# Expert layers of a two-layer mixer: plain fp32 products in column tiles, 16 landing pieces of two rows a partition

## The reference, cut to what matters

```python
N_EXPERTS = 16; EC_FACTOR = 2; D_EXPERT = D_MODEL = 1024

def expert_choice_ffn(h, router, w1, w3, w2):
    B, T, D = h.shape
    cap = max(1, EC_FACTOR * T // N_EXPERTS)
    aff = jax.nn.softmax(jnp.einsum('btd,de->bte', h, router).astype(jnp.float32), -1)
    gate, idx = lax.top_k(jnp.swapaxes(aff, 1, 2), cap)
    xs = jax.vmap(lambda hb, ib: hb[ib])(h, idx)
    hid = jax.nn.silu(jnp.einsum('becd,edf->becf', xs, w1)) * jnp.einsum('becd,edf->becf', xs, w3)
    ys = jnp.einsum('becf,efd->becd', hid, w2) * gate[..., None].astype(h.dtype)
    return jax.vmap(lambda yb, ib: jnp.zeros((T, D), yb.dtype).at[ib.reshape(-1)].add(yb.reshape(-1, D)))(ys, idx)
```

## Time and profile before

| | |
|---|---|
| median of 3 runs | 4865.87 us (4865.85 to 4869.79) |
| span of the profiled execution | 4858.5 us |
| between the two | 7.4 us |
| busy: PE, DVE, ACT, POOL | 86%, 64%, 39%, 10% |
| HBM read | 624.96 MB, 134 GB/s over the span |
| layer 0: first load, first product, last product's end | 717, 783, 1385 us |
| layer 1: the same | 2518, 2571, 3164 us |

### The profile page before, as it was taken

The page is one execution under the profiler, slowest core; times in us unless marked ns, Lnnn a source line. Parts: engine busy times, 40 slices in busy tenths (PEclk is TensorE's granted clock), DMA queues, the critical chain, the costliest instruction groups (busy, mean ns, idle before and its releaser), DMA issues. The chain is left out here.

```text
span 4858.5 us, 70272 instructions
## 1 busy us (share of the span) xinstructions
PE 4160.4 (86%) x28730; PEld 3310.1 (68%) x28730; DVE 3090.2 (64%) x4658; ACT 1887.0 (39%) x2558; POOL 481.2 (10%) x383
## 2 busy tenths in 40 slices
PE   7978876999978887979978999988989958697998
PEld 3855674666657774868854555587878748686877
DVE  6368957888864556656457888855467343574772
ACT  5122324667642312222125666634432222363221
POOL 0011000111101001414100111112000000100000
PEclk9987888999989997979788999999999977799999
DMA  7120026999960211000047999940122221002222
GB/s 274 35 90 26 1 89 244 356 349 370 369 218 34 69 54 57 3 6 3 23 164 283 358 364 361 327 125 1 36 101 94 91 67 37 1 2 70 95 96 78
DMA packets 254463, 658.45 MB, mean 136 GB/s; under 512 B 26884, under 2 KB 108036, under 8 KB 253624
## 3 DMA queue, kind: packets, MB, share of 16 engines
q1 hardware_dynamic: 240256, 614.97, 35.6%
q0 software_dynamic: 9216, 34.66, 2.6%
q10 hardware_dynamic: 4672, 4.33, 0.3%
HBM read 624.96 MB, written 28.41 MB: 134 GB/s over the span
## 5 line engine op out<-in xcount | busy, mean ns | idle before, releaser
L1843 DVE TENSOR_TENSOR w_lo<-w_quarter,w_hi 128x2048 fp32r<-128x2048 f32 x384 | 874.5, 2288 | 199.9 <-ACT w_hi L1766 198.6
L1766 ACT ACTIVATE w_hi<-w_quarter 128x2048 fp32r<-128x2048 f32 x384 | 735.5, 1918 | 378.7 <-DMA w_quarter<-in_moe_w 203.6
L3099 DVE TENSOR_TENSOR w_lo<-ffn_landing,w_hi 128x1024 fp32r<-128x1024 f32 x132 | 161.4, 1225 | 293.3 <-ACT w_hi L3077 293.3
L3051 PE MATMUL ffn_ps<-ffn_inT_hi,w_hi 128*128 128x512 f32 x704 | 276.4, 393 | 9.2 <-DVE w_lo L3099 9.2
L3051 PE MATMUL ffn_ps<-ffn_inT_lo,w_hi 128*128 128x512 f32 x704 | 276.0, 392 | 0.0
L3051 PE MATMUL ffn_ps<-ffn_inT_hi,w_lo 128*128 128x512 f32 x704 | 275.6, 391 | 0.0
L1343 ACT ACTIVATE prob<-score_ps,negmax 128x256 f32<-128x256 f32 (+4 forms) x272 | 166.4, 612 | 233.3 <-DVE negmax L1316 233.0
L1714 PE MATMUL down_ps<-w_hi,hiddenT 128*96 128x512 f32 (+1 forms) x512 | 207.0, 404 | 43.3 <-DVE w_lo L1843 32.1
L1651 POOL DMA_INDIRECT summed_dram<-gains_then_rows,row_token x32 | 118.3, 3696 | 1028.7 <-DVE gains_then_rows L1862 1028.7
L1714 PE MATMUL gate_ps<-w_hi,rowsT 128*96 128x512 f32 (+1 forms) x512 | 205.3, 401 | 12.7 <-DVE w_lo L1843 9.6
L1714 PE MATMUL up_ps<-w_hi,rowsT 128*96 128x512 f32 (+1 forms) x512 | 204.5, 399 | 6.2 <-DVE w_lo L1843 6.1
(11 more groups left out here) (680 smaller groups left out, 9811.3 us busy)
## 6 DMA issues: line engine op xcount, KB each, us to landing
w_quarter<-in_moe_w SPq DMA_DIRECT2D x384, 1024.0 KB, 6.8
ffn_landing<-in_f_w_up SPq DMA_DIRECT2D x88, 512.0 KB, 3.3
ada_landing<-in_ada_w SPq DMA_DIRECT2D x24, 1024.0 KB, 7.3
ada_ring<-in_ada_w SPq DMA_DIRECT2D x24, 1024.0 KB, 5.2
ffn_landing<-in_f_w_down SPq DMA_DIRECT2D x44, 512.0 KB, 3.3
w_landing<-in_od_w_in SPq DMA_DIRECT2D x13, 1024.0 KB, 10.6
w_landing<-in_a_w_in SPq DMA_DIRECT2D x12, 1024.0 KB, 6.0
w_landing<-in_ev_w_in SPq DMA_DIRECT2D x6, 1024.0 KB, 5.7
```

Source lines behind the costliest of these rows:

```text
L1766: nc.scalar.activation(wh[g % NP][:, :, :], land[g % NL][:, :, :], ACT.Copy).then_inc(hi_ready, 1)
L1843: tt(wl[g % NP][:, :, :], land[g % NL][:, :, :], wh[g % NP][:, :, :].bitcast(F32), ALU.subtract) \
L3051: mm = nc.tensor.matmul(ps[c % 4][:, :], w[:, c % NP, cols], h[:, k, :], start=(k + i == 0), stop=(k == KD - 1 and i == 2))
L3099: nc.vector.tensor_tensor(wl[:, c % NP, :], land[:, c % NL, :], wh[:, c % NP, :].bitcast(F32), ALU.subtract).then_inc(split, 1)
```

## The change

- The split is gone, and with it `wh`, `wl`, `hi_part`, `lo_part`, `turned_hi` and `turned_lo`. Products read the landed pieces as plain fp32. xs and hT have one buffer each, written by ACT (`rows_kept`) and DVE (`hidden_kept`).
- Products go in column tiles. For the 64 latent rows, half n of the output columns goes to partitions 64n to 64n + 63, in `out[:, 0:512]`. For the 32 context rows of layer 0, quarter n goes to partitions 32n to 32n + 31, in `out[:, 512:768]`. So hidden, y and the gain lie in that layout ("parts"), y is added by one indirect DMA of 128 half rows, and in layer 0 a second one of 128 quarter rows, with indices `pidx` worked out by DVE.
- 16 landing pieces. 10 in layer 0 and 12 in layer 1 are loaded at once; half of the others lie where nT is and wait for `scored`, half where h is and wait for `h_stored`. Later loads wait for `used`, PE's count of quarters. Their semaphores live through both layers (`landed`, `loaded`).
- A piece's rows are laid out as "(p k) n" instead of "(k p) n": a partition gets two neighbouring rows, 8 KB in one run, and the transposes pick rows and columns with a step of 2 to match.

```diff
+    LW, CW = D // 2, D // 4
+    W = LW + (CW if CR else 0)
+    NL = len(landed)
+    n_turn = nt // 2
+    n_free = NL - 2 * n_turn
...
-                    sp.wait_ge(split, g - NL + 1)
+                    sp.wait_ge(used, g - NL + 1)
-                sp.dma_start(land[g % NL][:, :, :], src.rearrange("(k p) n -> p k n", p=P)) \
+                sp.dma_start(land[g % NL][:, :, :], src.rearrange("(p k) n -> p k n", k=QK)) \
...
-            for g in range(NL):
+            for g in range(n_free):
                 load(g)
...
-            for g in range(NL, len(order)):
+            sp.wait_ge(scored, 1)
+            for g in range(n_free, n_free + n_turn):
                 load(g)
-            sp.wait_ge(y_added, 16 * E)
+            sp.wait_ge(h_stored, 16 * nt)
+            for g in range(n_free + n_turn, len(order)):
+                load(g)
+            sp.wait_ge(y_added, 16 * NS * E)
...
+                scatter(e, 0, lat_rows, slice(0, LW))
+                if CR:
+                    scatter(e, 1, ctx_rows, slice(LW, W))
...
             def quarter(out, v, g):
-                pe.wait_ge(split, g + 1)
-                q, c = order[g][2], g % NP
+                c = g % NL
+                pe.wait_ge(landed[c], 16 * (before[c] + g // NL + 1))
+                q = order[g][2]
                 for kk in range(QK):
                     k = q * QK + kk
...
                     for n in range(2):
-                        cols = slice(n * 512, (n + 1) * 512)
-                        nc.tensor.matmul(out[0:R, cols], v[0][:, k, :], wh[c][:, kk, cols], start=first, stop=False,
-                                         skip_group_check=True)
-                        nc.tensor.matmul(out[0:R, cols], v[0][:, k, :], wl[c][:, kk, cols], start=False, stop=False,
-                                         skip_group_check=True)
-                    for n in range(2):
-                        cols = slice(n * 512, (n + 1) * 512)
-                        mm = nc.tensor.matmul(out[0:R, cols], v[1][:, k, :], wh[c][:, kk, cols], start=False,
-                                              stop=last, skip_group_check=True)
+                        mm = nc.tensor.matmul(out[n * 64:(n + 1) * 64, 0:LW], v[:, k, 0:LR],
+                                              land[c][:, kk, n * LW:(n + 1) * LW], start=(k == 0), stop=(k == KD - 1),
+                                              skip_group_check=True)
+                for kk in range(QK if CR else 0):
+                    k = q * QK + kk
+                    for n in range(4):
+                        mm = nc.tensor.matmul(out[n * 32:(n + 1) * 32, LW:W], v[:, k, LR:R],
+                                              land[c][:, kk, n * CW:(n + 1) * CW], start=(k == 0), stop=(k == KD - 1),
+                                              skip_group_check=True, tile_position=(0, n * 32))
                 mm.then_inc(used, 1)
 
             def turn_hidden(e):
                 pe.wait_ge(hid_ready, e + 1)
...
+                for part in range(NS):
+                    for j in range(LW // P if part == 0 else CW // P):
+                        c = part * LW + j // QK * QK * P + j % QK
+                        mm = nc.tensor.transpose(misc[part][:, j * P:(j + 1) * P], hid[:, c:c + QK * P - 1:QK], ident)
...
-                pe.wait_ge(hid_kept, 2 * f + 2)
+                pe.wait_ge(hid_kept, NS * (f + 1))
+                if f:
+                    pe.wait_ge(y_ready, f)
...
+            def hidden_kept(e):
+                for part, n, r0, r in ((0, 2, 0, LR), (1, 4, LR, CR))[0:NS]:
+                    dve.wait_ge(hid_turned, NS * e + part + 1)
+                    nc.vector.tensor_copy(hT[:, :, r0:r0 + r].rearrange("p (n j) r -> p j n r", n=n),
+                                          misc[part][:, 0:KD * r].rearrange("p (j n r) -> p j n r", n=n, r=r)) \
+                        .then_inc(hid_kept, 1)
...
+            for part, n, r0, r in ((0, 2, 0, LR), (1, 4, LR, CR))[0:NS]:
+                nc.vector.tensor_copy(parts_v[:, part, :].rearrange("e (n r) -> e n r", n=n),
+                                      topv[:, r0:r0 + r].unsqueeze(1).broadcast_to([E, n, r]))
+                for j in range(n):
+                    last = nc.vector.tensor_scalar(parts_i[:, part, j * r:(j + 1) * r], topi[:, r0:r0 + r], float(n), float(j),
+                                                   ALU.mult, ALU.add)
```

More of the change, by code:

```diff
@@ L1541, in mixture @@
         st.sb("gains_of_the_stage_before", [P, 5, D])
[L1542 to L1545, removed]
+        land += [st.sb(f"w_quarter{c}", [P, QK, D]) for c in range(nt // 2, n_free)]
+        xs = st.sb("rowsT", [P, KD, R])
+        hT = st.sb("hiddenT", [P, KD, R])
         hid, shared, gain, shift = gains.hid, gains.shared, gains.gain, gains.shift
-        g2r = st.sb("row_gain", [R, D])
-        rows, ys = [shared[0:R, c, :] for c in range(2)], [shared[0:R, 2 + c, :] for c in range(2)]
+        g2r = st.sb("row_gain", [P, W])
+        rows, ys = [shared[0:R, c, :] for c in range(2)], [shared[:, 2 + c, 0:W] for c in range(2)]
         rw = st.sb("router", [P, KD, E])
@@ L1558, in mixture @@
         topi = st.sb("top_token", [E, R])
+        parts_v, parts_i = (left[:, c * NS * P:(c + 1) * NS * P].rearrange("e (s r) -> e s r", s=NS) for c in range(2))
         idx = st.sb("row_token", [R, E], mybir.dt.uint32)
-        gall = st.sb("row_gates", [R, E])
-        nT = st.sb("normedT", [P, KD, nt * P])
+        pidx = st.sb("part_row", [P, NS, E], mybir.dt.uint32)
+        gall = st.sb("part_gates", [P, NS, E])
+        with nc.sbuf_tensor(f"normedT_{i}", [P, KD, nt * P], F32) as nT:
+            pass
+        land += [st.sb(f"w_quarter{c}", [P, QK, D]) for c in range(n_free, n_free + n_turn)]
         with nc.sbuf_tensor(f"normed_rows_{i}", [P, nt, D], F32) as h:
             pass
-        wl = [st.sb(f"w_lo{c}", [P, QK, D], F32R) for c in range(NP)]
+        land += [st.sb(f"w_quarter{c}", [P, QK, D]) for c in range(n_free + n_turn, NL)]
         p1 = st.ps("gate_ps", [P, D])
@@ L1600, in mixture @@
         block = st.block()
+        before = list(loaded)
+        for g in range(len(order)):
+            loaded[g % NL] += 1
         def tile_rows(t, dram):
@@ L1637, in gather, with scatter @@
                     .then_inc(gathered[e % 2], 16)
+            def scatter(e, part, to, cols):
+                nc.gpsimd.indirect_dma_start(out=to,
+                                             out_offset=bass.IndirectOffsetOnAxis(ap=pidx[:, part, e:e + 1], axis=0),
+                                             in_=ys[e % 2][:, cols], in_offset=None, compute_op=ALU.add) \
+                    .then_inc(y_added, 16)
             pool.wait_ge(idx_ready, 1)
@@ L1649, in _ @@
                 if e:
[L1650 to L1653, removed]
+                    pool.wait_ge(y_added, 16 * NS * e)
+                scatter(e, 0, lat_rows, slice(0, LW))
+                if CR:
+                    scatter(e, 1, ctx_rows, slice(LW, W))
         @block.tensor
@@ new lines, in _ @@
+            last.then_inc(top_ready, 1)
+            dve.wait_ge(top_turned, 1)
+            nc.vector.tensor_copy(idx[:, :], misc[1][0:R, 0:E])
+            for part in range(NS):
+                c = (1 + 2 * part) * E
+                nc.vector.tensor_copy(pidx[:, part, :], misc[1][:, c:c + E])
+                last = nc.vector.tensor_copy(gall[:, part, :], misc[1][:, c + E:c + 2 * E])
+            last.then_inc(idx_ready, 1)
+            dve.wait_ge(idx_ready, 1)
+            dve.wait_ge(g2_landed, 16 * (6 if CR else 2))
@@ L1921, in _ @@
-                for q in range(GE + 1, GE + 3):
-                    lo_part(g0 + q)
-                rows_out(f, g0 + GE)
-            turned_lo(misc, RT, hT[0], hT[1], E - 1, hid_hi, hid_kept)
-            lo_part(G1 + GE * (E - 1) + 3)
+                hidden_kept(f)
+                hidden(f + 1, G1 + f * GE + 8)
+                rows_out(f, G1 + f * GE + GE)
+            hidden_kept(E - 1)
             rows_out(E - 1, G1 + GE * (E - 1) + 4)
@@ L3507, in build @@
                    for i, n in enumerate((NT, LT))]
+        landed = [nc.alloc_semaphore(f"quarter_landed{c}", num=Stage.LONG + 56 + c) for c in range(16)]
+        loaded = [0] * len(landed)
         lows = {0: beyond, 11: beyond + 6, 19: beyond + 12}
```

133 lines of the change are left out of this document (39 added, 94 removed).

## The result

The changed kernel takes 4749.56 us (median of 4 runs, 4740.87 to 4752.5), the kernel before 4865.86 beside it: ratio 0.9764, 95% interval 0.9742 to 0.9785. That is 116 us less, where 86 were forecast. Two executions, one of the last kernel in the table further down and one of the kernel before beside it, were slow (6081 and 11906 us) and count in no ratio.

The account below looks back on a forecast made before the run. In both layers DMA was taken as the limit by a little (2.89 us a quarter), PE right behind (2.77). Layer 0 -21 and layer 1 -64 sum to -85: 4866 to 4781, rounded 4780 us, range 4725 to 4815.

Parts of the forecast that it names:

- one wide load: na_bias, 28 KB a partition, moved 401 GB/s at share 0.93; taken as the upper end for 8 KB runs.
- Layer 1, -64 forecast: Second expert layer becomes one full stretch of DMA: 214.4 MB at 371 GB/s, 578 us, ending 3099.5 against 3164.
- saturated rate of 2700 to 3100, share 1.00: Kernel before, layer 1: 363 GB/s at DMA share 1.00, read as saturated; 2.89 us a quarter.
- 28.6 us of layer 0: PE's waits that end at DVE in layer 0, all that the split's removal was worth by itself.
- Rivals 1 and 2: Layer 1's rate: longer runs give nothing (363 GB/s, 4793 us, 0.15) or much (401 GB/s, 4738 us, 0.15).
- Layer 0, -21 forecast: First expert layer, ended by PE at 2.78 us a quarter: -23 us, with +2 us for scatters at its tail.
- rival 3: Layer 0's four 32-column tiles do not run at once; if only two do, +165 us, 4946 us; chance 0.09.
- the upper bound that I had kept: Layer 0, passage between tile shapes: 0.14 us a switch as upper bound, 0.10 taken.
- the last expert's turn of hidden: End of layer 0: the last expert's exposed turn of hidden, counted at 6 us.
- the 9 us left over: Layer 0: 9 us of the 602 measured not explained by the working (slow clock at start, gaps), kept in the forecast.
- rival 4: Layer 1: PE's clock stays at 1.2 GHz between landings, a quarter costs 3.44 us; 4971 us, chance 0.02.
- rival 5: Both layers: another step, such as a late gather, paces them, so nothing moves; 4866 us, chance 0.04.

Follow-up runs that it names:

- the last kernel in the table further down: Changed kernel with layer 0's 32-column products done for four quarters at once and paired rows in layer 1 alone: 4708.64 us, ratio 0.9651.
- The grouped kernels: Changed kernel with layer 0's 32-column products kept back and done together for two quarters (4726.75 us, 0.9677) or four (4709.74 us, 0.9641).

## Why the prediction held, and which term was mis-sized

The time fell into the range, and both layers ended as forecast, layer 0 by PE and layer 1 by DMA. The reason given for layer 1's rate was wrong. That its range still covered the measured rate is luck: its upper end was taken from one wide load, as the worth of long runs, which these turned out not to have.

**Layer 1, -64 forecast, -106 measured: the rate was the mis-sized term.** That DMA would be the limit, full from the first load on, and PE would leave the path, was right. So were the bytes: 51 x 388 + 491 x 396 = 214 MB, as forecast. The formula with the measured 400 GB/s, where I had taken 371, gives 214.4 / 0.400 = 536, from 2508 on 3044, plus 3: 3047; with 395, the mean from the first load on, it gives 3054. The last product started at 3047.7. But "saturated rate of 2700 to 3100, share 1.00" was the wrong reading. The share of 1.00 did not mean that the engines could move no more. In the kernel before, in 2600 to 3000 us, the SP queue waited for the split almost without a break:

```profile
SPq L1612 <- DVE w_lo L1843: 356.8, 133, 8.8
```

That row names who frees a piece, DVE's split; that this wait paced the loads it does not prove, since the queue waits 350 us at 399 GB/s too. The split put back with four and with eight pieces shows it. The prediction gave the split's removal only PE's waits for it, 28.6 us of layer 0, and nothing in layer 1; there, with the products cheap, it is worth 61.8. I read PE, ACT and DMA, and took SP's waits only at the start. Rivals 1 and 2 had the right ends, 363 and 401, for the wrong reason, the length of a run; that is worth 392 against 400. The kernel with 16 pieces moved 400 GB/s over 400 us, nearly all of it read from HBM. The Trainium skill (DMA: Bandwidth & Descriptors, Where 436 GB/s comes from) has the HBM side of a core bind at about 358; these traces disagree, and the kernel before did not stand at 358 to 363 for it, since it moved 374 with two more pieces. Another page of the skill (HBM Reference, Specifications (TRN2)) gives 358 as the share of a core whose neighbour streams too, and about 425 for a core alone, as this one is; with that the traces agree, in that 400 lies above the one and below the other.

Taken apart, from first to last product in layer 1: 591.8 to 580.2 with the cheap products and long runs, the split's wait still there; to 518.4 without that wait; to 487.4 with 16 pieces. More than half of the 104 us is the wait and some 30% the head start. The shares hold for this order of steps: the wait is worth this much only once the products are cheap. What the long runs are worth within the first step was not measured; their 10.6 us were measured with 16 pieces.

**Layer 0, -21 forecast, -16 measured.** PE ends it, as said. Four tiles of 32 columns do run at once: 64 records of 256 columns and one change of shape take 3.59 us, and 64 quarters of 0.215 are 3.44 (rival 3 falls). The quarter is 2.87, not 2.78: 1.87 and 1.00 where the products alone need 1.72 and 0.86, so 0.14 to 0.15 for each switch instead of 0.10, at the upper bound that I had kept; that is +17 us. The transposes' step of two, which I had priced at nothing, is another 6.6. The other side gave part of it back: the last expert's turn of hidden left 1.3 us instead of 6, and of the 9 us left over nothing is seen. The length is 585.6 against 578 forecast. The grouped kernels show that a change of shape costs PE 0.14 us; the Trainium skill (TensorEngine Tiling, Key Properties) has the rule that such a change drains the engine, without a price, and the trace agrees in that each change costs time.

**The clock** (rival 4) was granted at 0.98 in layer 1 despite 89 us of waits. **Nothing moves** (rival 5) fell with both layers.

The 7.6 us between the layers are scatter: in the 14 profiled executions here those stages, whose code is the same in all, took from 1115.6 to 1142.8 us. What makes them vary stays open.

## What to carry to other kernels

A DMA share of 1.00 is no proof that DMA is the limit, and a loading queue that waits nearly all the time for the consumer of a piece is no proof of the opposite. Ask who frees a piece, and count the loop: landing, each consumer in turn, release. If the number of pieces is small and the loop, divided by it, comes near the time that a piece takes in the layer, try two more pieces before anything else; here they alone gave 1.2%. It was a second limit close by, PE's, that kept this gain small, so price the next limit too. When fp32 products leave half of TensorE's columns idle, column tiles are what makes them pay (here 4775 us with them and 5060 without, both with four pieces), and products of one tile shape should be done in a row, since each change costs.

## What the runs showed of the hardware

- The DMA share read 1.00 or more at 363, 368, 374, 392 and 400 GB/s in stretches of this case, so by itself it doesn't tell whether more could be moved.
- SP's queue waited 356, 350 and 349 of 400 us at 364 GB/s (4 pieces, split back), 399 (4 pieces) and 396 (8 pieces, split back).
- One core's DMA engines moved 400 GB/s for 400 us, weights above all.
- Plain fp32 in two tiles of 64 columns and in four of 32 lost no time to sharing: 32 records of 512 columns took 7.02 us and 64 of 256 took 3.59, each with one change of shape. A change between the two cost 0.14 us.
- Copies and subtractions of 128 x 2048 fp32 on ACT and DVE, busy 73 and 87% of the time, left the landings at 394 GB/s where there were 399 without, in one execution each, and at 400 in the last 100 of the 400 us.
- A transpose of 96 rows with a step of two between its columns took 0.152 us instead of 0.115.
